# Two chained transformer blocks on one core: turning the mixed expert tokens tile by tile, and three changes of waits and order

## The reference

```
# first block
z = rms_norm(x) * (1 + sc1) + sh1 ; proj = z @ w_in
w_low, a_low -> decay = f(w0 + tanh(w_low) @ w2), a = sigmoid(a0 + a_low @ a2)     # "low rank"
rwkv7_mixer(r, k, v, decay, a, ...)        # kk = k*k_k / sqrt(sum(kk*kk)) per head, then the recurrence
x = x + gt1 * (gated sum of both mixers @ w_o)
x = x + gt2 * ((silu(conv(h @ w_up)_gate) * conv(h @ w_up)_val) @ w_down)           # 2816 hidden channels
x = rms_norm(x)
# second block
h = modulated rms_norm(x) ; proj = h @ w_in_2        # q_lat, kv_lat, k_rope, q_b, k_b, v_b, gates
q_a = rope(rms_norm(q_lat) @ w_uq) ; k_nope, v_a = rms_norm(kv_lat) @ w_uk, w_uv
mla_attend(...) ; chunk_band_attend(q_b, k_b, v_b, rel_table)   # scores/8 + bias[distance], masked by chunk
x = x + gt1 * merged @ w_out
y = sum over the 2 chosen of 32 experts, weight * expert(token)
x = x + gt2 * y ; return rms_norm(x) * g_final
```

## Time and profile before

| What | Value |
|---|---|
| Times of the runs, us | 2435.66, 2436.11, 2439.73 (median 2436.11) |
| The profiled execution: its own time / its span, us | 2438.35 / 2436.5 |
| Mean granted TensorE clock | 0.957 of full speed |
| Busy share PE / PE weight loads / DVE / ACT / POOL | 91% / 65% / 47% / 30% / 9% |
| Chain that ended last, share of the span | PE 75%, DVE 10%, ACT 4%, DMA 4%, unknown queue 2% |

### The profile page before, as it was taken

How to read it: one execution, slowest core, us unless ns; L and a number is a source line. 1 busy time by engine, 2 the same in 40 slices (tenths; PEclk the granted TensorE clock), 3 DMA queues, 4 the chain that set the end, 5 groups by cost and what they waited for, 6 DMA issues and landing times.

```text
span 2436.5 us, 41213 instructions
## 1 busy us (share of the span) xinstructions
PE 2216.9 (91%) x17720; PEld 1581.3 (65%) x17720; DVE 1144.0 (47%) x2011; ACT 738.5 (30%) x1107; POOL 217.7 (9%) x97
## 2 busy tenths in 40 slices
PE   7989899999989999988899998977899999699994
PEld 5385858595436889665678886856645677466662
DVE  4445454543656655245467772253254543511113
ACT  2323232321431222353343331151234532322222
POOL 0020202020000000000134343410000000000001
PEclk9999999999989999999999999988999999899997
DMA  7201010102456556102323332244020133479994
GB/s 252 69 21 37 20 53 4 53 4 89 147 163 228 184 159 197 35 1 87 87 73 100 86 99 68 93 83 133 26 87 18 44 96 108 180 291 409 404 412 148
DMA packets 216315, 295.27 MB, mean 121 GB/s; under 512 B 7640, under 2 KB 191872, under 8 KB 207968
## 3 DMA queue, kind: packets, MB, share of 16 engines
q1 hardware_dynamic: 210784, 274.85, 33.4%
q0 software_dynamic: 3072, 9.74, 1.9%
q10 hardware_dynamic: 2304, 8.39, 0.8%
HBM read 279.84 MB, written 13.11 MB: 120 GB/s over the span
## 4 chain that ended last, share of the span: by engine, by line
PE 75%; DVE 10%; ACT 4%; DMA 4%; issue 3%; another core or an unknown queue 2%; SPq 1%; POOL 1%; POOLq 0%; DVEq 0%; ACTq 0%
PE ps L1146 10%; PE ps L766 10%; PE ps L659 9%; PE ps L987 7%; PE ps L955 6%; PE ps L1175 5%; PE ps L1355 4%; PE ps L1011 3%; PE ps L1328 2%; PE ps L1041 2%; PE ps L1057 2%; PE ps L1376 2%; PE ps L1128 2%; DMA ring<-in_w_up 2%
## 5 line engine op out<-in xcount | busy, mean ns | idle before, releaser
L766 PE MATMUL ps<-arena 64*64 64x64 f32 x7168 | 227.5, 222 | 15.0 <-POOL arena L1909 8.8
L766 PEld LDWEIGHTS ps<-arena 64*64 64x64 f32 x7168 | 222.4, 138 | 19.7 <-POOL arena L1909 9.8
L659 PE MATMUL ps<-hT,ring 128*128 128x512 f32 (+1 forms) x480 | 212.8, 601 | 3.1 <-ACT hT L1428 2.4
L1915 POOL TENSOR_TENSOR w_low<-ring,w_high 128x2048 fp32r<-128x2048 f32 x22 | 102.0, 4636 | 824.9 <-ACT w_high L1670 824.9
L659 PEld LDWEIGHTS ps<-hT,ring 128*128 128x128 f32 (+1 forms) x480 | 90.8, 190 | 122.3 <-issue 119.8
L1146 PE MATMUL ps<-h_high,w_low 128*128 128x512 f32 x352 | 140.0, 398 | 7.3 <-DVE h_low L2330 7.3
L1146 PE MATMUL ps<-h_low,w_high 128*128 128x512 f32 x352 | 140.6, 399 | 0.0
L1146 PE MATMUL ps<-h_high,w_high 128*128 128x512 f32 x352 | 140.0, 398 | 0.0
L1454 ACT ACTIVATE arena<-ps 128x512 f32<-128x512 f32 x104 | 62.1, 597 | 213.5 <-PE ps L766 203.2
L2236 DVE CUSTOM_DVE_ANT_0 arena<-ps,arena 128x256 f32<-128x256 f32 (+3 forms) x160 | 67.0, 468 | 123.7 <-PE ps L1057 123.6
L2053 DVE TENSOR_TENSOR arena<-ps,arena 128x512 f32<-128x512 f32 x88 | 60.9, 692 | 118.7 <-PE ps L766 118.6
(11 more groups left out here) (410 smaller groups left out, 4407.6 us busy)
## 6 DMA issues: line engine op xcount, KB each, us to landing
ring<-in_w_in SPq DMA_DIRECT2D x54, 1024.0 KB, 5.3
arena<-in_w_ada SPq DMA_DIRECT2D x80, 512.0 KB, 4.0
arena<-in_w_down SPq DMA_DIRECT2D x32, 1024.0 KB, 9.1
ring<-in_w_gate SPq DMA_DIRECT2D x30, 1024.0 KB, 9.6
ring<-in_w_up SPq DMA_DIRECT2D x30, 1024.0 KB, 10.8
ring<-in_w_up SPq DMA_DIRECT2D x44, 512.0 KB, 5.0
ring<-in_w_down SPq DMA_DIRECT2D x8, 1024.0 KB, 5.0
y_scratch<-arena ACTq DMA_DIRECT2D x16, 512.0 KB, 7.8
```

The source lines that it names most:

```text
L659: mm = pe.matmul(dst, w[:, k, hf * P:hf * P + width], rhs(k), start=(start and k == 0), stop=(stop and k == kts - 1))
L766: mm = pe.matmul(ps[r, bank, cc], l[r, cc], x[r, 0:64] if x is eye64 else x[r, cc], start=(i == 0), stop=(i == len(terms) - 1))
L1915: pool.tensor_tensor(W_LOW[:, slot_, :], ring[:, slot_, :], W_HIGH[:, j % 2, :].bitcast(F32), ALU.subtract).then_inc(w_low, 1)
```

## The change

1. **End of the experts.** `mixed` becomes four semaphores, one for each token tile. PE turns token tile by token tile, each as soon as it is mixed, all eight channel tiles into eight different banks (`MIX_BANK`). The sums of the squares come after all turns, when DVE has emptied bank 6.
2. **Bias tiles.** The wait for `got_bias` and the eight multiply-adds leave in2; head `h`'s stands behind the rotation of head `h` in lat2, with the wait at `h == 0`.
3. **Down waits.** PE no longer waits for all 22 hidden tiles and all of DVE's PSUM work before the first down matmul; output half 0 waits for hidden tile by hidden tile, and each bank for its own emptying.
4. **Low-rank order.** In each quad the halves 0 and 1 come ahead of the `lora` products; the waits for `lora_ready` and `got_lora` move behind them in quad 0, and the drain there becomes a wait for each bank.

```diff
-        mixed, mix_turned, ... = [...]
+        mixed = [sem(f"mixed_{i}") for i in range(4)]
+        MIX_BANK = (6, 0, 1, 2, 3, 4, 5, 7)
...
-            pe.wait_ge(lora_ready, 1)
-            pe.wait_ge(got_lora, 32)
...
             for q in range(4):
+                def projected(m, hf, i):
+                    hh = q * 6 + i
+                    if hh >= 4:
+                        pe.wait_ge(freed["D"], BEFORE["rkv"]["D"] + hh - 3)
+                    elif hh < 3:
+                        pe.wait_ge(freed["D"], BEFORE["lora"]["D"] + hh + 1)
+                    half(m, hf, hh % 4, h_)
+                m = slot()
+                projected(m, 0, 0)
+                projected(m, 1, 1)
                 if q == 0:
-                    drain_psum(pe, "rkv")
+                    pe.wait_ge(lora_ready, 1)
+                    pe.wait_ge(got_lora, 32)
                 for s in range(2):
...                 (the lora products)
-                m = slot()
-                projected(m, 0, 0)
-                projected(m, 1, 1)
                 m = slot()
                 projected(m, 0, 2)
...
-            pe.wait_ge(hidd, FT)
-            drain_psum(pe, "down")
...
+                        elif part == 0:
+                            pe.wait_ge(freed["D"], BEFORE["down"]["D"] - (2 if hh < 2 else 0))
                         for k in range(kts):
                             kt = part * 8 + k
+                            if hh == 0:
+                                pe.wait_ge(hidd, kt + 1)
...
-            pe.wait_ge(mixed, rounds * 4)
-            for k in range(KT):
-                if k >= 2:
-                    pe.wait_ge(freed["D"], BEFORE["moe"]["D"] + k - 1)
-                for tt in range(4):
-                    mm = pe.transpose(ps[:, 2 + k % 2, tt * P:tt * P + P], GX[:, tt, k * P:k * P + P], ident)
-                mm.then_inc(mix_turned, 1)
-                if k >= 3:
-                    norm_sum(5, k - 3, k - 2)
-            norm_sum(5, 5)
+            for tt in range(4):
+                pe.wait_ge(mixed[tt], rounds)
+                for k in range(KT):
+                    mm = pe.transpose(ps[:, MIX_BANK[k], tt * P:tt * P + P], GX[:, tt, k * P:k * P + P], ident)
+                    if tt == 3:
+                        mm.then_inc(mix_turned, 1)
+            pe.wait_ge(freed["D"], BEFORE["moe"]["D"] + 1)
+            norm_sum(5)
...
-            def bias_tiles(h0):
-                dve.wait_ge(got_bias, 16)
-                for h in range(h0, h0 + 4):
-                    lk.done(stt(BT[:, h, :], BT[:, h, :], 8.0, CH, ALU.mult, ALU.add))
...
-                if o in (1, 3):
-                    bias_tiles(2 * o - 2)
...
                 lk.done(tt(QA[r, h, :], QA[r, h, :], ROT[r, h % 2, :], ALU.add))
+                if h == 0:
+                    dve.wait_ge(got_bias, 16)
+                lk.done(stt(BT[:, h, :], BT[:, h, :], 8.0, CH, ALU.mult, ALU.add))
...
-                stt(xT[:, k, :], ps[:, 2 + k % 2, :], ...
+                stt(xT[:, k, :], ps[:, MIX_BANK[k], :], ...
```

More of the change, by code:

```diff
@@ L380, in build @@
         fetched = [sem(f"fetched{i}") for i in range(4)]
-        mixed, mix_turned, round_link, half_mixed, round_held = [sem(n) for n in ("mixed", "mix_turned", "round_link", "half_mixed", "round_held")]
+        mixed = [sem(f"mixed_{i}") for i in range(4)]
+        MIX_BANK = (6, 0, 1, 2, 3, 4, 5, 7)
+        mix_turned, round_link, half_mixed, round_held = [sem(n) for n in ("mix_turned", "round_link", "half_mixed", "round_held")]
         out_scaled = sem("out_scaled")
@@ L1887, in _ @@
                                       YO[:, j, :]).then_inc(y_stored[j], 16)
-                act.wait_ge(mixed, r * 4 + 4)
+                for tt in range(4):
+                    act.wait_ge(mixed[tt], r + 1)
             for k in range(KT):
@@ L2598, in mix_second @@
                 stt(GX[:, tt_, :], GY[:, 2 * tt_ + 1, :], WGT_IN[:, 2 * tt_ + 1:2 * tt_ + 2], GX[:, tt_, :],
-                    ALU.mult, ALU.add).then_inc(mixed, 1)
+                    ALU.mult, ALU.add).then_inc(mixed[tt_], 1)
             with dve.Fori(0, rounds) as r:
@@ L2637, in _ @@
                 dve.wait_ge(mix_turned, k + 1)
-                stt(xT[:, k, :], ps[:, 2 + k % 2, :], mod2[:, 40 + k:41 + k], xT[:, k, :], ALU.mult, ALU.add).then_inc(freed["D"], 1)
+                stt(xT[:, k, :], ps[:, MIX_BANK[k], :], mod2[:, 40 + k:41 + k], xT[:, k, :], ALU.mult, ALU.add).then_inc(freed["D"], 1)
             dve.wait_ge(rooted, 6)
```

## The result

The changed kernel took 2412.95 us in the median of its first four runs (2401.56 to 2414.36), against 2436.1 before; the ratio is 0.9892, 95% interval 0.986 to 0.9923, so it is about 1% faster. In a second series, beside some of the experiments, it took 2417.05 against 2438.89, ratio 0.9907 [0.9889, 0.9925]. The forecast was 2409.6 in a range of 2403 to 2418. The profiled execution has a span of 2412.6, 23.9 less than before.

What follows compares the result with a forecast made beforehand. PE, busy 91% and holding 75% of the chain, was taken as the bound, so only its waits count. 12.4 + 11.6 + 3.3 - 0.8 = 26.5 us gave 2409.6 us from 2436.11, range 2403 to 2418.

Steps and rivals of the forecast that it cites:

- In2: Fifth slot: PE's 12.85 us gap shrinks to 2.1, set by ring load, cast and subtraction; gain 12.4 us.
- a sign of being wrong: In2: the prediction would be wrong if a clock at 1.2 GHz followed the 2.1 us gap.
- My step from the length of a gap to the clock behind it: In2: clock stays up behind 2.1 us, since 2.25 us was followed by 1.00 and 2.57 by 0.66.
- The lower end: In2: gain of 10.7 us if the clock falls behind the remaining gap, against 12.4 if not.
- The transfers: In2: by the turn-taking rule a slow write and the ring load slow each other; load still late, gain still 12.4.
- a fast load: In2: a ring load landing in 5.3 us would give some 2 us more; left untested.
- Bias adds in lat2: Lat2: eight adds of 0.72 us fit DVE's 1.24 us idle per head; price 0, or 5.8 without cover.
- Down: Start of down: the 9.17 us wait and the slow start behind it go; gain 11.6 us, bounds 9.2 and 11.7.
- Quad 0 and quads 1 to 3: Low-rank order: root 5.1 us earlier in quad 0, 2.0 later in each other quad, 5.9 together; net loss 0.8.
- The drain that the Trainium skill puts beside each table load: Quads: 1.38 us beside each 1.28 us load would cost up to 2.8 a quad more, time near 2419.
- The end: End of the experts: turning tiles as they are mixed ends the sums earlier; gain 3.3 us, bounds 2.7 and 4.5.
- The sum: Whole kernel: all terms together gain 26.5 us, median time 2409.6.

Runs made afterwards that it cites:

- the second trace: The changed kernel profiled again with nothing altered, in a second series; 2417.05 us against 2438.89 for the kernel before, span 2417.9.
- experiment 8: All four edits, low-rank order in quad 0 only, bias write held until three in2 slots are done; 2424.8 us, ratio 0.9932 to the kernel before.
- 9: All four edits, low-rank order in quad 0 only, bias write from 128 partitions in place of 8; 2396.66 us, ratio 0.9834 to the kernel before.
- 10: The kernel before with only the bias write taken from 128 partitions; 2417.81 us, ratio 0.9924 to the kernel before.
- experiment 5: The kernel before with only the low-rank order, in quad 0 alone, quads 1 to 3 as before; 2435.61 us, ratio 0.9985.

## Why the prediction was right, point by point

**In2.** The mechanism held: load, cast, subtraction, PE. Forecast 12.4 us, measured 11.6 from down to kv in the profiled pair, 12.4 in the second trace (169.4). The 11.6 flatter the forecast. In2 itself, from its first split matmul to its last, went from 91.2 to 82.5 us, and the norm in front of it gave 0.9; the other 2.0 came behind in2 (65.8 to 63.8 us to kv), where a PE gap of 2.15 us was followed by a clock of 0.69 before and 1.00 here. That is luck. In the second trace in2 itself gave 12.1. Two things moved. The gap was 3.08 and not 2.1 us, because the norm in front of in2 was 0.9 us shorter (from down's last matmul to in2's first 23.9 us, before 24.8) while the load's landing hangs on the bias write, which starts with the norm; what the gap grew by, the norm had given. And the clock fell behind it, which the prediction had named as a sign of being wrong: the mechanism of the gap held, the clock behind it did not. My step from the length of a gap to the clock behind it was not safe: gaps of 2.38, 2.39 and 2.53 us at this place were followed by full speed, those of 2.35 and 3.08 by the low clock. The trace of the kernel before could have warned me. I took two gaps from it; it has eleven of 1.9 to 2.6 us, and in the 3 us behind nine of them the granted clock was 0.50 to 0.72. One of the nine, right behind down, is as short as the 2.25 us of the earlier trace rows (PE's timeline and the window behind it):

```profile
1604.42 2.07 PE L683 MATMUL ps<-hT,const 128*128 128x512 f32 x2 [2.24 <-DVE hT L2304]
...
1604.40:1607.40 3.00, 2.07 (x2) 0.50 (x2) 0.00 (x0) 1.39 (x3) 1.12 (x2) 0.50 1.09 382
```

The lower end was too high as well: for in2 itself the five traces with the bias edit and the slow write give 8.7, 10.5, 11.9, 12.1 and 12.1 us, the first of them below the 10.7 (below it also with the norm's 0.9), because a longer gap came together with the low clock.

**The transfers.** The prediction could not tell whether the write slowed the loads. Experiments 8, 9 and 10 tell: with the write 9.1 instead of 55 us long the loads land in 5.4. The rule of the Trainium skill (DMA: Bandwidth & Descriptors, Queues, rings and completion order), that a DMA engine takes turns between queues with work, fits: a 1 MB load beside a write of 2.5 MB took up to 25.8 us before, and the chain of experiment 8 has 46.58 us of such a load. The forecast's estimate that a fast load would give some 2 us more came out at 2.9. The prediction took the slow write as given; that it is slow by how its source is laid out, and that the whole wait hangs on this, it did not see.

**Bias adds in lat2:** priced at 0, measured at 0, with 0.51 us of cover left.

**Down:** forecast 11.6, measured 11.7. Nothing of the slow start was left.

**Quad 0 and quads 1 to 3.** Forecast +5.1 and -5.9, net -0.8. The root in quad 0 came at 95.21, forecast 95.5; the root of quad 1 4.3 us behind the halves, forecast 4.1. By the distances of experiment 5, quad 0 gave 4.6 us in the mean (forecast 5.1) and quads 1 to 3 cost 2.12 each, 6.4 together (forecast 5.9). Net, the profiled pair shows a gain of 0.5 and the order alone a ratio of 1.001: within the noise of nothing, as forecast. The drain that the Trainium skill puts beside each table load (ScalarE: Activation LUTs, What ACT_TABLE_LOAD costs) did not show in the changed kernel either: from the load at 205.34 to the scaling at 209.24 are 3.9 us, room for the load and four sigmoids only. (The prediction's time by that page is also mis-added: three quads at 2.8 us more give 2418, not 2419.)

**The end:** forecast 3.3, measured 2.8 to 2.9 over all traces, 3.4 in the profiled pair. The prediction wrote 3.60 / 4 as 0.86 us for a sum; it is 0.90, and the eight took 7.11 us, 0.89 each.

**The sum:** 26.5 forecast; the edits gave 27.2 in the profiled pair, of which 2.0 were the luck behind in2, and 3.7 us in the gate stage went the other way. That the total came within 3.4 us of the forecast median owes something to such pieces cancelling. The forecast had no term for chance of the clock in stages that aren't touched, though single executions of the changed kernel lie up to 12.8 us apart (2401.56 to 2414.36). The mean granted clock of the four executions follows their times: 0.970 for the 2401.56, and 0.966, 0.964 and 0.964 for the 2412.01, 2413.90 and 2414.36. In which stages the fastest one had its higher clock is open, since it has no trace.

## What to carry to other kernels

Price a moved wait by what is late next: the bias wait hid a slow transfer behind it, which then set the gap. When a side transfer takes long, look at how many partitions it reads from, and at the busy share of the DMA engines meanwhile, before moving what waits for it; here the same bytes from 128 in place of 8 partitions gave more than the reordering, and left it nothing to give. Before taking the clock behind a gap from one like it, list all gaps of about that length in the trace. An order that is good where an engine idles (quad 0) can cost where it does not (quads 1 to 3); make it only where the gap is.

## What the runs showed of the hardware

A write of 2.5 MB from 8 partitions in 1024 pieces took 55 us at a DMA share of 0.49, from 128 partitions 9 us at 0.93. Two gaps of PE of the same length, at the same place in quad 2, were followed by different clocks, 0.68 in the kernel before and 1.00 in the changed one (PE's timeline and the window behind it, before and then changed):

```profile
367.55 4.73 PE L766 MATMUL ps<-const,arena 64*64 64x64 f32 x102 [3.04 <-DVE arena L2103]
...
367.00:372.00 5.00, 4.45 (x102) 4.48 (x104) 1.00 (x2) 1.63 (x4) 0.00 (x0) 0.68 0.01 3
```

```profile
366.34 5.81 PE L766 MATMUL ps<-const,arena 64*64 64x64 f32 x192 [3.05 <-DVE arena L2106]
...
366.00:371.00 5.00, 4.66 (x159) 4.69 (x161) 0.79 (x2) 2.61 (x5) 0.00 (x0) 1.00 0.01 3
```

That is why quad 2 hid its loss in the changed kernel: the 224 matmuls behind the gap took 6.76 us in the chain, before 8.31. It may not be all chance: the quad 2 gap was followed by 1.00 in all three traces with the full order, and in one of the eleven others. Over the four quads of the 14 traces, this gap of 3.04 or 3.05 us was followed by 1.00 in 7 of 56 cases and by 0.50 to 0.71 in the rest, taken over the 5 us behind it. What decides it is open. One untouched stretch alone varies by 8 us between executions, so a difference of that size between single executions of this kernel needs a table by stretch before it is put down to an edit.
